# Transformer block pair: the first scale and shift made as columns on two engines, with two projection chunks between their parts

## The reference

```
cond = silu(c)                                   # 2048 numbers
mod = cond @ w_ada + b_ada                       # w_ada: 2048 x 12288
sh1, sc1, gt1, sh2, sc2, gt2 = split(mod, 6)     # 2048 each
h = rms_norm(x, g_pre_mix) * (1 + sc1) + sh1     # x: 256 x 2048
p = h @ w_in + b_in                              # w_in: 2048 x 9216
u, v, q, k, v_att, z_pool, gates = split(p)      # 6 branches of 512, gates of 6144
```

## Time and profile before

| | us |
|---|---|
| median of three executions | 3102.84 |
| profiled execution, device time | 3099.53 |
| its span | 3097.7 |
| TensorE busy | 2984.4 (96%) |
| VectorE busy | 1817.7 (59%) |
| ScalarE busy | 1261.6 (41%) |
| mean granted TensorE clock | 0.983 |

### The profile page before, as it was taken

The page is one execution under the profiler, slowest core; times in us unless marked ns, Lnnn a source line. Parts: engine busy times, 40 slices in busy tenths (PEclk is TensorE's granted clock), DMA queues, the critical chain, the costliest instruction groups (busy, mean ns, idle before and its releaser), DMA issues.

```text
span 3097.7 us, 43155 instructions
## 1 busy us (share of the span) xinstructions
PE 2984.4 (96%) x18048; PEld 2589.3 (84%) x18048; DVE 1817.7 (59%) x1777; ACT 1261.6 (41%) x1207; POOL 326.1 (11%) x465
## 2 busy tenths in 40 slices
PE   8899999997999999999898999998999999999998
PEld 3488777886999999888687888877889999999886
DVE  1376777787777776544445447664555555555444
ACT  0143455435545444344433434434444343443343
POOL 1000000000000000000104918720000000000000
PEclk9999999998999999999898999999999999999999
DMA  9776777895666655566546662225655555555554
GB/s 362 277 275 263 279 282 286 301 350 204 235 228 244 231 206 189 206 210 211 192 141 189 216 210 92 80 86 192 243 186 181 192 196 195 190 191 208 211 209 170
DMA packets 109853, 666.49 MB, mean 215 GB/s; under 512 B 23472, under 2 KB 25680, under 8 KB 33296
## 3 DMA queue, kind: packets, MB, share of 16 engines
q1 hardware_dynamic: 101584, 626.96, 56.5%
q0 software_dynamic: 8144, 37.74, 3.3%
HBM read 647.26 MB, written 17.39 MB: 215 GB/s over the span
## 4 chain that ended last, share of the span: by engine, by line
PE 91%; DVE 3%; DMA 2%; ACT 2%; issue 1%; POOL 0%; SPq 0%; DVEq 0%; ACTq 0%; POOLq 0%
PE acc L1976 27%; PE acc L1977 27%; PE acc L1978 27%; PE ms L2050 3%; PE tp L2025 1%; DVE w_lo L1244 1%; DMA ada<-ada_stream 1%; DMA w_raw<-w_stream 1%; PE ms L2427 0%; DMA w_raw<-ada_stream 0%; PE acc L2466 0%; PE acc L2456 0%; ACT w_hi L783 0%; PE ms L2426 0%; ACT bias_rows L914 0%
## 5 line engine op out<-in xcount | busy, mean ns | idle before, releaser
L1244 DVE TENSOR_TENSOR w_lo<-w_raw,w_hi 128x2048 fp32r<-128x2048 f32 x484 | 1110.2, 2303 | 733.1 <-ACT w_hi L783 714.6
L783 ACT ACTIVATE w_hi<-w_raw 128x2048 fp32r<-128x2048 f32 x484 | 922.6, 1915 | 985.8 <-DMA w_raw<-w_stream 982.8
L1976 PE MATMUL acc<-h2T_hi,w_lo 128*128 128x256 f32 x2816 | 785.1, 279 | 0.0
L1977 PE MATMUL acc<-h2T_lo,w_hi 128*128 128x256 f32 x2816 | 784.2, 278 | 0.0
L1978 PE MATMUL acc<-h2T_hi,w_hi 128*128 128x256 f32 x2816 | 784.2, 278 | 0.0
L1976 PEld LDWEIGHTS acc<-h2T_hi,w_lo 128*128 128x128 f32 x2816 | 532.0, 189 | 0.1
L1977 PEld LDWEIGHTS acc<-h2T_lo,w_hi 128*128 128x128 f32 x2816 | 531.5, 189 | 0.0
L1978 PEld LDWEIGHTS acc<-h2T_hi,w_hi 128*128 128x128 f32 x2816 | 531.0, 189 | 0.0
L1976 PE MATMUL acc<-w_hi,hid_lo 128*128 128x512 f32 x704 | 275.0, 391 | 5.9 <-DVE w_lo L1244 5.9
L1978 PE MATMUL acc<-w_hi,hid_hi 128*128 128x512 f32 x704 | 274.6, 390 | 0.0
L1977 PE MATMUL acc<-w_lo,hid_hi 128*128 128x512 f32 x704 | 274.5, 390 | 0.0
(11 more groups left out here) (515 smaller groups left out, 3930.5 us busy)
## 6 DMA issues: line engine op xcount, KB each, us to landing
w_raw<-w_stream SPq DMA_DIRECT2D x484, 1024.0 KB, 4.8
ada<-ada_stream SPq DMA_DIRECT2D x64, 1024.0 KB, 6.9
w_raw<-ada_stream SPq DMA_DIRECT2D x32, 1024.0 KB, 5.0
g_dram<-gates_out SPq DMA_DIRECT2D x12, 512.0 KB, 6.9
gates_in<-g_dram POOLq DMA_DIRECT2D x12, 512.0 KB, 6.3
bias_rows<-b_in POOLq DMA_DIRECT2D x18, 256.0 KB, 6.1
x_res<-x POOLq DMA_DIRECT2D x2, 2048.0 KB, 14.2
g_dram<-gate_stage SPq DMA_DIRECT2D x8, 512.0 KB, 6.1
```

The lines of the kernel that those rows point to most:

```text
L783: sc.activation(whi[:, s % 4], raw[:, s % 4], ACT.Copy).then_inc(hi_made, 1)
L1244: v.tensor_tensor(wlo[:, s % 4], raw[:, s % 4], whi[:, s % 4].bitcast(F32), ALU.subtract).then_inc(lo_made, 1)
L1976: mm(o, sl, mh, start=start, stop=False, skip_group_check=share)
L1977: mm(o, sh, ml, start=False, stop=False, skip_group_check=share)
```

## The change

- TensorE makes only `sc1`, VectorE only `sh1`. The 16 groups of `sc1` get four buffers of their own (`ada_first`); the 16 of `sh1` go through `ada1` and `ada_group`. TensorE's part now has the weight tile as the stationary operand and one column of `cond` moving (`first_mods`), so its result is a column per 128 outputs, as is that of `first_product`.
- x is scaled with the reciprocal root, transposed at once into `xT`, and scale and shift are applied to the transposed x as columns: ScalarE writes the high part, VectorE computes the same value into `x_mod` and subtracts (`first_rows`).
- This goes by quarters c of the 2048 input rows. Between the parts of quarter c+1, TensorE runs group c of chunk 0 and group c of chunk 1 (`N_EARLY` = 8 groups, interleaved, so that both chunks end with the last quarter).
- SP interleaves the loads: per four pairs of `sc1` and `sh1` groups two weight groups.
- The 36 later ada groups no longer come ahead of every second split from 2 to 72, but ahead of splits 8, 9, 10, 12, ..., 66, 67, 68, 70, 71, 72 (`SIDE`); the load of r+2 is issued when TensorE has finished weight group `SIDE[r]`, the first two when it has finished groups 5 and 6. Products, their columns, and the small steps of gating and pooling are shifted by one to three groups; the transposed copy of the `gt1` columns is written earlier and alone.

```diff
-ROUNDS1 = ["mod0", "ws0", "ws1", "mod1", ...
+ROUNDS1 = ["ws0", "ws1", "mod0", "sgu0", ...
+N_EARLY = 8
+SIDE = [8, 9] + list(range(10, 67, 2)) + [67, 68, 70, 71, 72]
...
@@ SP
-            for j in range(4):
-                load(j, a["ada_stream"][j])
-            with sp.Fori(1, N_FRONT // 4) as i:
...
+            def first(p):
+                n, h = divmod(p, 2)
+                src = a["ada_stream"][h * 4 * GK + n]
+                if h:
+                    if n >= 2:
+                        sp.wait_ge(mod_used, n - 1)
+                    load_ada(ada1, n % 2, src)
+                else:
+                    if n >= 4:
+                        sp.wait_ge(ada_used, n - 3)
+                    sp.dma_start(adaf[n % 4][:].rearrange("p k c -> p (k c)"), src).then_inc(first_in[n % 4], 16)
+            def early(s):
+                if s >= 4:
+                    sp.wait_ge(pe_used, s - 3)
+                load(s % 4, a["w_stream"][s % 2 * 4 + s // 2])
+            for p in range(N_FRONT):
+                first(p)
+                if p >= 7 and p % 4 == 3:
+                    early(p // 4 - 1)
+            early(N_EARLY - 1)
+            for s in range(4, G_IN1):
                 sp.wait_ge(pe_used, s + 1)
                 load(s % 4, a["w_stream"][s + 4])
-                r = s // 2 - 1
-                if s % 2 == 0 and s and r + 2 < A_IN:
-                    sp.wait_ge(mod_used, r + 1)
-                    load_ada(ada1, r % 2, a["ada_stream"][N_FRONT + r + 2])
+                if s in (5, 6):
+                    sp.wait_ge(mod_used, A_FIRST - 6 + s)
+                    load_ada(ada1, s - 5, a["ada_stream"][N_FRONT + s - 5])
+                for r in range(A_IN - 2):
+                    if SIDE[r] == s:
+                        sp.wait_ge(mod_used, A_FIRST + r + 1)
+                        load_ada(ada1, r % 2, a["ada_stream"][N_FRONT + r + 2])
...
@@ ScalarE
+            for r in range(KD // 2):
+                act.wait_ge(tp_full, r + 1)
+                sc.activation(xflat[:, r * C:(r + 1) * C], tp[r % 2][:], ACT.Copy).then_inc(tp_free[r % 2], 1)
+            for c in range(4):
+                act.wait_ge(sem("mod_evac"), c + 1)
+                for k in range(GK * c, GK * c + GK):
+                    ins = sc.activation(h1T[0][:, k], xT[:, k], ACT.Identity, scale=acol[:, k:k + 1], bias=scol1[:, k:k + 1])
+                ins.then_inc(sem("h1_hi"), 1)
+                split()
+                split()
...
@@ VectorE
+            def first_rows(c):
+                dve.wait_ge(sem("shifts"), c + 1)
+                k = slice(GK * c, GK * c + GK)
+                v.tensor_tensor(scol1[:, k], ms[c % 2][:, GK:2 * GK], bcol[:, 1, k], ALU.add)
+                chain(v.tensor_tensor(acol[:, k], ms[c % 2][:, 0:GK], bcol[:, 0, k], ALU.add))
+                chain(v.scalar_tensor_tensor(acol[:, k], acol[:, k], 1.0, pcol[:, k], ALU.add, ALU.mult))
+                dve.sem_inc(sem("mod_evac"), 1)
...
+                for i in range(GK):
+                    kk = GK * c + i
+                    ins = v.tensor_scalar(xm[:, i], xT[:, kk], acol[:, kk:kk + 1], scol1[:, kk:kk + 1], ALU.mult, ALU.add)
+                chain(ins)
+                dve.wait_ge(sem("h1_hi"), c + 1)
+                v.tensor_tensor(h1T[1][:, k], xm[:], h1T[0][:, k].bitcast(F32), ALU.subtract).then_inc(sem("h1"), 1)
+            dve.wait_ge(sem("cond"), 1)
+            first_shifts(0, GK)
+            rstd_wait()
+            for t in range(TT):
+                v.tensor_scalar(x[:, t], x[:, t], rstd[:, t:t + 1], None, ALU.mult).then_inc(sem("xn"), 1)
+            for c in range(4):
+                if c < 3:
+                    first_shifts(GK * (c + 1), GK * (c + 1) + 2)
+                first_rows(c)
+                split()
+                if c < 3:
+                    first_shifts(GK * (c + 1) + 2, GK * (c + 2))
+                split()
...
             def to(s):
                 while m.n <= s:
-                    r = m.n // 2 - 1
-                    if m.n % 2 == 0 and r < A_IN:
+                    if m.n in SIDE:
+                        r = SIDE.index(m.n)
                         ada_group(ada1, macc1[r // 4 % 2], r % 4)
                     split()
...
@@ TensorE
+            def first_mods(c, g0, g1):
+                if c >= 2 and g0 == 0:
+                    pe.wait_ge(sem("mod_evac"), c - 1)
+                for g in range(g0, g1):
+                    n = c * GK + g
+                    pe.wait_ge(first_in[n % 4], (n // 4 + 1) * 16)
+                    for q in range(GK):
+                        k = g * GK + q
+                        for f in range(4):
+                            ins = mm(ms[c % 2][:, f:f + 1], adaf[n % 4][:, q, f * P:(f + 1) * P], cond[:, k:k + 1],
+                                     start=k == 0 and f == 0, stop=k == KD - 1, skip_group_check=True)
+                    ins.then_inc(ada_used, 1)
+            def first_product(c):
+                pe.wait_ge(mod_acc, c + 1)
+                for f in range(4):
+                    ins = mm(ms[c % 2][:, GK + f:GK + f + 1], macc1[c % 2][:, f * P:(f + 1) * P], ones[:], start=True, stop=True)
+                ins.then_inc(sem("shifts"), 1)
...
+            first_mods(0, 0, GK)
+            first_product(0)
+            pe.wait_ge(sem("xn"), TT)
+            for k in range(KD // 2):
+                turn([(x[:, t, (2 * k + q) * P:(2 * k + q + 1) * P], q * S + t * P) for q in range(2) for t in range(TT)])
+            for c in range(4):
+                for n in range(2):
+                    if c < 3:
+                        first_mods(c + 1, 2 * n, 2 * n + 2)
+                    if n == 0:
+                        pe.wait_ge(sem("h1"), c + 1)
+                    rows_group(bank(n), h1T, c)
+                if c < 3:
+                    first_product(c + 1)
```

More of the change, by code:

```diff
@@ L197, in block_program @@
         gb1 = [u(f"gates_in{j}", [P, TT, C], 32 + 4 * j) for j in range(3)]
-        h1 = u("h1", [P, TT, D], 56)
+        adaf = [u(f"ada_first{j}", [P, GK, C], 40 + 8 * j) for j in range(4)]
+        xT = u("xT", [P, KD, S], 72)
+        xm = u("x_mod", [P, GK, S], 100)
         tril = u("tril", [P, P], 88)
-        row1, rowT1 = u("row1", [P, 2, D], 32), u("rowT1", [P, D], 48)
         y3T = [u("y3T_hi", [P, 3, 4, S], 64, F32R), u("y3T_lo", [P, 3, 4, S], 76, F32R)]
@@ L297, in block_program @@
         ada_in = [sem("ada_in0"), sem("ada_in1")]
+        first_in = [sem(f"first_in{i}") for i in range(4)]
         mod_used, mod_acc, mod_sum = sem("mod_used"), sem("mod_acc"), sem("mod_sum")
@@ L885, in _ @@
                     to(b + 5 + 2 * n)
+                    if (hp, n) == (2, 0):
+                        r = R1["mod_rows1"]
+                        act.wait_ge(tp_full, r + 1)
+                        chain(sc.activation(modr1[0:D // P], tp[r % 2][0:D // P, 0:P], ACT.Copy))
+                        act.sem_inc(tp_free[r % 2], 1)
+                        act.sem_inc(sem("mod_rows"), 1)
                     exps(sc1, w)
@@ L1285, in scaled @@
                 return v.scalar_tensor_tensor(dst, src, rstd[:np_, c:c + 1], row, ALU.mult, ALU.mult)
[L1288 to L1306, removed]
             adas = Tally()
@@ L2038, in _ @@
             pe.wait_ge(sem("cond"), 1)
[L2039 to L2055, removed]
-                mods()
-            pe.wait_ge(sem("ld_ident"), 16)
-            for n in range(4):
-                pe.wait_ge(sem("h1"), 2 * n + 2)
-                for k in range(2 * n, 2 * n + 2):
-                    turn([(h1[:, t, (2 * k + q) * P:(2 * k + q + 1) * P], q * S + t * P) for q in range(2) for t in range(TT)])
-            turned()
-            sums = Tally()
+            def first_mods(c, g0, g1):
[15 more added lines that the diff above has]
+                ins.then_inc(sem("shifts"), 1)
             def rows_group(b, xT, g):
@@ L2126, in _ @@
             pe.wait_ge(sem("ones"), 1)
-            to(7)
-            product(0)
-            to(9)
+            to(10)
             pe.wait_ge(sem("sguw_m"), 1)
@@ L2133, in _ @@
                 turn([(wsn[:, 4 * r + q], q * P) for q in range(4)])
-            to(12)
+            to(11)
+            product(0)
+            to(14)
             copied(R1["ws0"])
@@ L2141, in _ @@
                 ins.then_inc(sem("sgu_mix"), 1)
-            to(15)
-            product(1)
-            to(16)
+            to(18)
             pe.wait_ge(sem("y_sgu"), 1)
@@ L2152, in _ @@
             pooled(0)
-            to(19)
+            to(21)
             pool_y(0)
-            to(20)
+            to(22)
             pooled(1)
-            to(22)
+            to(23)
             pool_y(1)
-            to(23)
-            product(2)
             def qk_turn(hp):
@@ L2207, in _ @@
                     pv1(hp - 1, 3)
-                if hp == 3:
-                    product(6)
+                if hp == 1:
+                    product(3)
                 to(b + 2)
@@ L2212, in _ @@
                 to(b + 3)
```

(12 more changed lines are left out.)

124 lines of the change are left out of this document (63 added, 61 removed).

## The result

| kernel | median, us (range, runs) | ratio to before, 95% | profiled span | granted clock |
|---|---|---|---|---|
| before | 3103.24 (3101.33 to 3104.11, 4) | | 3097.7 | 0.983 |
| after | 3125.36 (3121.99 to 3129.53, 4) | 1.0069 [1.0057, 1.0081] | 3120.2 | 0.969 |

The change makes the kernel 22 us slower. In the profiled executions it is 3121.99 against 3099.53, 22.5 us; the medians differ by 22.1. The forecast was +12.9.

The account below looks back on a forecast made before the run. TensorE, busy for 96% of the span, was taken as the bound. The front's -10.6 us and the late ada loads' +23.5 gave +12.9, or 3116 us against the median; own range 3103 to 3127, with both main cases 3078 to 3125.

Parts of the forecast that it names:

- both main cases: The forecast (chance 0.52) and the rival of one-column products at full clock (0.33), held by the range 3078 to 3125.
- the ends of the halves: Front: five stretches of two one-column `sc1` groups and a weight group, 17.5 us each, ends 15.1 to 23.3.
- the ends of the stalls: Later ada groups: TensorE's waits with the low clock behind them, value 23.5 us, ends 15 and 35.
- The clock under one-column products: Front: clock falls in each `first_mods` run, rises in the weight group behind; granted 0.6 to 0.8, records 0.20 us apart.
- rival 1: Front: one-column products hold the full clock; group 8 starts at 141 us, time 3083 us; chance 0.33.
- Rival 2: Front: clock falls but does not slow weight loads, spacing 0.10; group 8 at 152, time 3093 us; chance 0.08.
- The front: From the start to group 8: group 8 starts at 175.4 us, 10.6 us earlier than before.
- the turns: Front, ahead of the first half: eight rounds of transposes of four tiles each, 0.97 us a round, to 44 us.
- the bare chain: Before group 6: quarter 3's columns, scaling and split with no `sc1` products to cover them, 7.1 us.
- The late ada loads: Loads issued too late for splits 9, 10, 67, 68, 71 and 72: waits of 20.6 us, plus 3 of low clock.
- The shifted steps: Moved steps of gating, pooling and attention: zero, hidden by the 5.44 us groups; up to 2 us if one comes late.
- Behind group 72 nothing changes: From the start of weight group 72 to the end: same work before and after, difference 0.

Follow-up runs that it names:

- e1: After, with each scale product of TensorE moving 64 equal columns of cond instead of one; 3097.72 us, ratio to before 0.9989.
- e2: After, with each later ada load issued one weight group earlier (the first two behind groups 3 and 5); 3104.59 us, ratio to before 1.0008.
- e5: e3 with VectorE's addition of the fourth column product moved behind the normalised scores; 3072.77 us, ratio to before 0.9904.
- e7: After with all four edits: 64 columns, early loads, fourth column addition behind the scores, shift products ahead of the group; 3068.36 us, ratio to before 0.9893.
- e9: e3 with 32 columns instead of 64; 3104.33 us, ratio to before 1.0002.
- e4: e3 with VectorE's addition of the fourth column product moved behind the maximum of the scores; 3075.38 us, ratio to before 0.9925.
- e10: e3 with 16 columns instead of 64; 3104.05 us, ratio to before 1.0013.
- e3: After with both edits, 64 columns moving and later ada loads issued one weight group earlier; 3076.19 us, ratio to before 0.9912.
- e6: e3 with TensorE's shift products put ahead of the second weight group of each half; 3070.34 us, ratio to before 0.9888.

## Why the prediction was right

The direction and both mechanisms came out as forecast, the size less well: 3116 forecast, 3125.4 measured, inside the forecast's own range of 3103 to 3127 and 0.4 us above the 3125 that closes the range for both main cases. That it lies inside is in part luck. The own range holds the ends of the halves alone, -12 to +12.5 us; with the ends of the stalls, -8.5 to +11.5, at the same time it would be 3095 to 3140. And 6.2 of the 9.6 us that the profiled difference exceeds the forecast by arose where nothing was forecast. By its steps:

- **The clock under one-column products.** Right. 0.50 in 47 to 54, 0.69 over 81 to 160, 0.68 over 45 to 160 (forecast 0.6 to 0.8). The first quarter's 128 records took 27.47 us, 0.215 each (forecast 0.20). e1 shows the clock as the cause: with it rival 1's front returns, all but 5.8 us. TensorE waited for no load between 43 and 160 us, the sign that would have made all of it wrong. Rival 2 (weight loads not slowed) falls by the 0.215.
- **The front.** Right as a sum, group 8 at 175.38 (forecast 175.4), but that the sum fits so closely is luck, for its parts are off and cancel: the first quarter, its product and x ended 1.9 us later (36.97 against 35.1), the turns took 6.9 and not 8.9; group 0 began at 54.65 and not at 57; five halves from 62.80 to 155.15, without the two products of 0.8 us between them, took 90.7 us, 18.1 each (forecast 17.5); the bare chain took 6.90 (forecast 7.1).
- **The late ada loads.** The mechanism right, the sum near, the places partly off. TensorE's waits at groups 9 and 10 were 3.43 and 1.17 (forecast 1.7 to 2 and 5.2: the first was larger and took from the second); around 67 and 68, 2.63 and 1.27 (1.3 and 5.9); 2.50 before group 71 (1.7), 4.49 and 0.54 before group 72 (4.7). Together 16.0 us against 20.6. The low clock was more than the 3 us put in: 26.9 less these 16.0 and the 2.84 at group 44 leaves 8 us. e2 took 15.2 us out of the stretch.
- **The shifted steps: "zero ... up to 2 us if one comes late".** Wrong. One came late: 2.84 us of waiting at group 44 and low clock behind it. I looked at the distance in groups between steps and not at what is queued behind VectorE's wait. In e5 and e7 it is gone.
- **Group 8 to 72 in all**: +26.9 us, forecast +23.5.
- **"Behind group 72 nothing changes".** Off by 6.2 us (2521.1 against 2515.0). Some 1.8 are group 72's own first products at the low clock, after the wait in front of it. In two places more the clock was low 3.4 us longer than before, worth at most 1.7 us each: from 705.3 to 708.7 it is 0.50 where before has 1.00 at the same distance from group 72, and the 0.50 from 1541.6 on lasts 20.4 us and not 17.0. The rest, about 1 us, is not traced. All that is beyond group 72's own products is no fixed cost of the change: in kernels with its work the stretch took 2515.0 in e9, 2515.3 in e4, 2515.8 in e5 and e7, 2518.8 in e10 and 2521.6 to 2522.9 in e1, e2, e3 and e6. What differs where I looked is when the clock falls and rises: e3 has 0.50 from 1859.1 to 1876.2, e7 has 1.00 at the same distance from group 72. What decides it is open.

In one line: -10.6 + 26.9 + 6.2 = +22.5 us, where -10.6 + 23.5 + 0 = +12.9 was forecast.

## What to carry to other kernels

Cheap instructions are not cheap time on TensorE if they take its clock away: price a long run of thin products at the low clock, look at the granted clock of that stretch first, and try the same products with more columns before anything else; here 64 columns instead of one cost nothing and gave back 25 to 28 us, while 16 and 32 gave nothing. But look at the clock ahead of them too: the same 64 columns ran at the spacing of the low clock in the first quarter, 0.215 us a record. When work is moved onto a list of steps, check for each step how far ahead its load is issued and which instructions stand behind its wait on the same engine, not only how far apart the steps are.

## What the runs showed of the hardware that was not expected

- Going from one column to 32 changed the granted clock of 81 to 160 us from 0.69 to 0.68, going to 64 changed it to 0.92 to 0.94. I had expected a slope. And 64 columns kept a full clock but did not raise a low one: 128 records took 27.57 us in e1 from 7.89 on, and 64 took 7.26 from 43.41 on, behind the transposes.
- 32 dense transposes with no weight group around them were followed by a rise of the clock. They took 6.90 us, 0.216 each, which is nearer to the cold spacing of the earlier trace rows (1.94 for 8) than to the warm one (1.04); behind them the window of after has 0.94, before it falls to 0.50 under the one-column products:

```profile
43.00:47.00 4.00, 4.00 (x36) 3.86 (x34) 3.28 (x7) 1.27 (x3) 0.00 (x0) 0.94 1.01 426
```

The rule that I drew on in the prediction (the Trainium skill, "TensorE: Matmul & The Clock Gate", Part 4, that transposes do not count as busy in the same way) does not hold for this stretch; it did for the 134 to 138 us of before, where the transposes had gaps between them. What tells the two apart no run here tested. In e7 the rise shows within the transposes: the first 16 took 3.37 us, 0.21 each, the next eight 1.14.

```profile
37.08 3.37 PE L2080 MATMUL tp<-ident,x_res 128*128 128x128 f32 x16
40.67 1.14 PE L2080 MATMUL tp<-ident,x_res 128*128 128x128 f32 x8 [0.22 <-ACT xT L834]
```

Ahead of 43 us the profile of after gives 1.00 although the spacing is that of the low clock, so there the spacing is the better witness.
